# Gate weight tiles placed between the steps of the second attention, with two shared PSUM banks

## The reference

```python
z = hn @ w_in
q_a, k_a, v_a, q_b, k_b, v_b, f_logit, g_a, g_b = jnp.split(z, split_idx, axis=-1)
a = moba_attention(...)            # 8 heads; over 256 tokens causal, with a bias linear in distance
bfx = forgetting_attention(...)    # 8 heads; causal, bias from the cumulated log forget gate
a = merge_heads(a) @ w_proj_a
bfx = merge_heads(bfx) @ w_proj_b
merged = jax.nn.sigmoid(g_a) * a + jax.nn.sigmoid(g_b) * bfx
x = x + merged @ w_out
```

## Time and profile before

| | us |
|---|---|
| median of 3 runs | 3013.37 |
| lowest, highest | 3007.05, 3026.69 |
| the profiled execution | 3013.09 |
| its span | 3011.3 |
| TensorE busy | 2830.1 |
| VectorE busy | 1782.6 |
| ScalarE busy | 1153.4 |

### The profile page before, as it was taken

One profiled execution on the slowest core, in us unless ns is written; L12 is line 12 of the kernel. 1 busy time (PEld: TensorE's weight loads), 2 busy tenths in 40 slices (PEclk: granted clock), 3 DMA queues, 4 the chain that ended last, 5 costly groups with the idle time before them and its releaser, 6 DMA issues.

```text
span 3011.3 us, 33804 instructions
## 1 busy us (share of the span) xinstructions
PE 2830.1 (94%) x12624; PEld 2270.3 (75%) x12624; DVE 1782.6 (59%) x1999; ACT 1153.4 (38%) x1487; POOL 398.4 (13%) x299
## 2 busy tenths in 40 slices
PE   5899998879899999999989998999999999999997
PEld 2477777558778888888767886788787888888886
DVE  2368883475688755555574445545454565556565
ACT  2122222344434444444343444444344444434443
POOL 1215530000377400000070000000000000000000
PEclk9999999899999999999999999999999999999998
DMA  8778783116677655555536551465555565655552
GB/s 308 283 237 303 266 304 123 42 56 214 231 251 265 236 185 193 187 189 192 171 126 222 190 192 38 168 196 194 168 182 168 194 196 181 195 187 188 188 189 98
DMA packets 279977, 579.30 MB, mean 192 GB/s; under 512 B 9585, under 2 KB 12368, under 8 KB 277336
## 3 DMA queue, kind: packets, MB, share of 16 engines
q1 hardware_dynamic: 272128, 540.71, 53.9%
q0 software_dynamic: 7440, 37.43, 3.5%
q10 hardware_dynamic: 328, 0.09, 0.0%
HBM read 572.92 MB, written 5.27 MB: 192 GB/s over the span
## 4 chain that ended last, share of the span: by engine, by line
issue 58%; PE 21%; DVE 7%; POOLq 6%; DMA 2%; POOL 2%; ACT 2%; DVEq 2%; ACTq 0%; SPq 0%
PE bank L365 5%; PE bank L366 5%; PE bank L367 5%; DVE proj_ctx L1444 3%; POOLq L2057 2%; PE bank L625 2%; POOLq L2059 2%; DMA w_raw<-in_w_ada 1%; DVE w_lo L361 1%; POOLq L2066 1%; DVEq L1443 1%; POOLq L2064 1%; PE bank L1756 1%; PE bank L658 1%; ACT probs L732 1%
## 5 line engine op out<-in xcount | busy, mean ns | idle before, releaser
L361 DVE TENSOR_TENSOR w_lo<-w_raw,w_hi 128x1024 fp32r<-128x1024 f32 (+1 forms) x856 | 1117.8, 1328 | 652.6 <-ACT w_hi L353 640.3
L353 ACT ACTIVATE w_hi<-w_raw 128x1024 fp32r<-128x1024 f32 (+1 forms) x856 | 891.7, 1054 | 1278.0 <-PE bank L367 1146.4
L365 PE MATMUL bank<-w_hi,xa_hi 128*128 128x512 f32 (+1 forms) x2304 | 910.3, 395 | 35.9 <-DVE w_lo L361 24.6
L367 PE MATMUL bank<-w_hi,xa_lo 128*128 128x512 f32 (+1 forms) x2304 | 900.2, 391 | 0.0
L366 PE MATMUL bank<-w_lo,xa_hi 128*128 128x512 f32 (+1 forms) x2304 | 900.0, 391 | 0.0
L365 PEld LDWEIGHTS bank<-w_hi,xa_hi 128*128 128x128 f32 x2304 | 436.4, 189 | 148.1 <-issue 32.6
L367 PEld LDWEIGHTS bank<-w_hi,xa_lo 128*128 128x128 f32 x2304 | 435.7, 189 | 90.5
L366 PEld LDWEIGHTS bank<-w_lo,xa_hi 128*128 128x128 f32 x2304 | 436.7, 190 | 88.1 <-issue 0.7
L365 PE MATMUL bank<-w_hi,ffn_act_hi 128*128 128x512 f32 x864 | 339.3, 393 | 7.8 <-DVE w_lo L361 7.8
L366 PE MATMUL bank<-w_lo,ffn_act_hi 128*128 128x512 f32 x864 | 338.1, 391 | 0.0
L367 PE MATMUL bank<-w_hi,ffn_act_lo 128*128 128x512 f32 x864 | 338.0, 391 | 0.0
(11 more groups left out here) (283 smaller groups left out, 1904.2 us busy)
## 6 DMA issues: line engine op xcount, KB each, us to landing
w_raw<-in_w_in SPq DMA_DIRECT2D x116, 1024.0 KB, 5.0
w_raw<-in_w_ada SPq DMA_DIRECT2D x80, 1024.0 KB, 5.8
w_raw<-in_w_up SPq DMA_DIRECT2D x64, 1024.0 KB, 5.2
w_raw<-in_w_down SPq DMA_DIRECT2D x64, 1024.0 KB, 5.1
w_raw<-in_ffn_wg SPq DMA_DIRECT2D x44, 1024.0 KB, 5.1
w_raw<-in_ffn_wu SPq DMA_DIRECT2D x44, 1024.0 KB, 5.2
w_raw<-in_ffn_wd SPq DMA_DIRECT2D x44, 1024.0 KB, 5.1
w_raw<-in_w_out SPq DMA_DIRECT2D x32, 1024.0 KB, 5.1
```

The lines of the kernel that those rows point to most:

```text
L353: act.activation(whi[:, slot, ks, 0:w], raw[:, q, ks, 0:w], ACT.Copy)\
L361: dve.tensor_tensor(wlo[:, slot, ks, 0:w], raw[:, q, ks, 0:w], whi[:, slot, ks, 0:w].bitcast(F32), ALU.subtract).then_inc(sem("lo_made"), 1)
L365: pe.matmul(out, xh, wh, start=first, stop=False)
L367: return pe.matmul(out, xl, wh, start=False, stop=last)
```

## The change

- The eight tiles of the first quarter of g_a and g_b are taken by halves in steps 0 to 15 of the second attention (`gate_half`), one half a step, between the scores and the transposes of the probabilities. They go to banks 1 and 7.
- To free these, keys and queries of all heads share bank 0, and the outputs of all heads bank 6. So TensorE's transposes of head n wait for the copies of head n-1, not n-2, and the output of a head waits for out_lo of the head before.
- The split of tile 0 stands ahead of step 0 on ScalarE and VectorE, that of tile n/2+1 at the end of the even steps 0 to 12.
- The sigmoids of g_a's quarter are issued by ScalarE at the end of step 8, those of g_b's at the end of step 16; TensorE waits for the former before half tile 8, since g_b uses the same banks.
- In the second attention out_lo goes from the middle of VectorE's step to its head.
- The buffer of gate values moves by 8 KB. `merge(0, True)` keeps only the projection tiles. The first attention (`wide()`) stays as it was.

The core of the diff (what is left out are lines of the sigmoid buffer and of the unchanged first attention):

```diff
-        sig = at("gate_sig", [P, 4, NCH], F32, 160)
+        sig = at("gate_sig", [P, 4, NCH], F32, 168)
...
-            for j in range(k):
+            for j in range(k) if js is None else js:
...
-                return ps[0][:, :] if self.wide() else ps[a % 2][:, 0:SEQ]
+                return ps[0][:, :] if self.wide() else ps[0][:, 0:SEQ]
...
-                return ps[1][:, :] if self.wide() else ps[a % 2][:, SEQ:2 * SEQ]
+                return ps[1][:, :] if self.wide() else ps[0][:, SEQ:2 * SEQ]
...
+            def o_bank(self, d):
+                return ps[6 + d % 2] if self.wide() else ps[6]
...
-                    wait(pe, T + "_qk_copied", A.since(s["a"]))
+                    wait(pe, T + "_qk_copied", s["a"])
...
+                if not A.wide() and n < 2 * 8:
+                    gate_half(pe, U, n // 2, n % 2)
...
-                    wait(pe, T + "_out_lo", d - 1)
-                    o = ps[6 + d % 2]
+                    wait(pe, T + "_out_lo", d - 1 if A.wide() else d)
+                    o = A.o_bank(d)
...
-                if 0 <= q < 3:
+                if 0 <= q < 3 and A.wide():
...
+        GATE_BANKS = (ps[1], ps[7])
+
+        def gate_half(pe, U, u, half):
+
+            if u == 4 and half == 0:
+                pe.wait_ge(sem("gate_sigmoid"), 1)
+            unit(pe, U // 4 + u // 4, u % 4, GATE_BANKS, XA, 4 * (u % 4), u % 4 == 0, u % 4 == 3,
+                 js=(2 * half, 2 * half + 1))
+
+        def next_gate(n):
+
+            return n // 2 + 1 if n % 2 == 0 and n // 2 + 1 < 8 else None
+
+        def sigm_1(act, U, b):
+
+            used(act, U + 4 * b + 4)
+            for tk in range(2):
+                m = act.activation(sig[:, 2 * b + tk, :], GATE_BANKS[tk][:, :], ACT.Sigmoid, scale=stat(RSTD + tk))
+            m.then_inc(sem("gate_sigmoid"), 1)
...
+            if not A.wide():
+                hi(act, U // 4, 0)
...
-                q = next_unit(n, hi_)
+                q = next_unit(n, hi_) if A.wide() else next_gate(n)
                 if q is not None:
-                    hi(act, U // 4, q)
+                    hi(act, U // 4 + q // 4, q % 4)
+                if not A.wide() and n in (8, 16):
+                    sigm_1(act, U, n // 16)
...
+            if not A.wide():
+                lo(dve, U // 4, 0)
             for n in range(lo_, hi_ + 4):
+                if not A.wide():
+                    out_lo(dve, A, n, lo_, hi_)
...
-                for b in range(first, 2):
+                for b in () if first else range(2):
```

More of the change, by code:

```diff
@@ L367, in mm3, with unit @@
             return pe.matmul(out, xl, wh, start=False, stop=last)
-        def unit(pe, u4, q, outs, X, k0, first, last, k=KQ, w=NCH, toks=(0, 1), slot=None, follow=0):
+        def unit(pe, u4, q, outs, X, k0, first, last, k=KQ, w=NCH, toks=(0, 1), slot=None, follow=0, js=None):
             slot = q % 2 if slot is None else slot
-            for j in range(k):
+            for j in range(k) if js is None else js:
                 if j % (k // 2) == 0:
@@ L673, in attn_pe @@
             pe.wait_ge(sem(T + "_out_lo"), 16)
-            pe_next(pe, A, U, k0s, 3)
+            if A.wide():
+                pe_next(pe, A, U, k0s, 3)
+        GATE_BANKS = (ps[1], ps[7])
[11 more added lines that the diff above has]
+            m.then_inc(sem("gate_sigmoid"), 1)
         def pe_next(pe, A, U, k0s, q):
@@ L709, in attn_act @@
                         act.wait_ge(sem(T + "_out"), s["d"] + 1)
-                    act.activation(A.X[0][:, srcs_of(s)["o"], :], ps[6 + s["d"] % 2][:, out_cols(s)],
+                    act.activation(A.X[0][:, srcs_of(s)["o"], :], A.o_bank(s["d"])[:, out_cols(s)],
                                    ACT.Copy).then_inc(sem(T + "_out_hi"), 1)
@@ L743, in attn_act, with out_lo @@
                     m.then_inc(sem("diff_squares"), 1)
-                q = next_unit(n, hi_)
+                q = next_unit(n, hi_) if A.wide() else next_gate(n)
                 if q is not None:
-                    hi(act, U // 4, q)
+                    hi(act, U // 4 + q // 4, q % 4)
+                if not A.wide() and n in (8, 16):
+                    sigm_1(act, U, n // 16)
+        def out_lo(dve, A, n, lo_, hi_):
+            for s in outputs_of(A, n, lo_, hi_):
+                dve.wait_ge(sem(A.tag + "_out_hi"), s["d"] + 1)
+                o = srcs_of(s)["o"]
+                dve.tensor_tensor(A.X[1][:, o, :], A.o_bank(s["d"])[:, out_cols(s)],
+                                  A.X[0][:, o, :].bitcast(F32), ALU.subtract).then_inc(sem(A.tag + "_out_lo"), 1)
         def attn_dve(dve, A, lo_, hi_, U):
@@ L825, in attn_dve @@
                         m.then_inc(sem("diff_normed"), 1)
-                q = next_unit(n, hi_)
+                q = next_unit(n, hi_) if A.wide() else next_gate(n)
                 if q is not None:
-                    lo(dve, U // 4, q)
+                    lo(dve, U // 4 + q // 4, q % 4)
         A1 = Attn("att", STEPS, 4, kT, qT, probs, probsT, XA)
@@ L1350, in merge @@
                 g = 3 * n + U_MRG // 4
[L1351 to L1357, removed]
+                if not first:
+                    for q in range(4):
+                        hi(act, g, q)
+                    hi(act, g + 1, 0)
+                    hi(act, g + 1, 1)
+                    sigm(n, 0)
+                    hi(act, g + 1, 2)
+                    hi(act, g + 1, 3)
                 hi(act, g + 2, 0)
                 hi(act, g + 2, 1)
-                sigm(n, 1)
+                if not first:
+                    sigm(n, 1)
                 hi(act, g + 2, 2)
@@ L1680, in merge @@
                     lo(dve, g, 3)
-                for q in range(4):
-                    lo(dve, g + 1, q)
+                    for q in range(4):
+                        lo(dve, g + 1, q)
                 for q in range(4):
```

## The result

The changed kernel takes 3029.93 us (median of 20 runs, 3015.48 to 3037.62) against 3011.95 us (20 runs) for the kernel before on the same chips. The ratio is 1.0055, with a 95% interval of 1.004 to 1.007: a loss of 12 to 21 us.

A forecast was written before the change was run, and what follows sets the result against it. TensorE, busy 94% of the span, bounds the kernel, but a ScalarE-VectorE loop bounds biased steps. Start about 4, step 8 some 12 and the tail the rest make +16.8 us: 3013.1+16.8=3029.9, about 3030 us; 8-in-10 range 3010 to 3042.

The forecast's parts named there:

- the loop and not TensorE bounds biased steps: Biased steps of the second attention: the ScalarE-VectorE loop takes 12.92 us a pair, against 10.66 us by TensorE.
- Wins half a microsecond a pair: Biased pairs of steps: 4.90 us are added to save 5.44 us later.
- step 8 waits for the sigmoids: Step 8: TensorE waits 9.7 us for banks 1 and 7 to be read by the sigmoids, last in ScalarE's step.
- the half tile at the low clock: Step 8, behind the wait: granted clock about 0.50, so the half tile takes 5.44 instead of 2.72 us.
- The dense forget-gate steps and their zero: Steps 9 to 15: TensorE bounds them at 7.05 us each; 2.72 us added and 2.72 us saved per step.
- The tail: Steps 16 to 19, left without gate tiles beside them: a chain of 19.3 us from step 15's end to the projection tiles.
- about 13 us of idle TensorE: Sign of a right forecast: the tail shows this much TensorE idle time, with granted clock 0.5.
- the third table load: ScalarE's switch back to exponentials in step 9: it lies in a wait for VectorE whatever a switch costs.
- a granted clock under 1 in steps 3 to 7: Sign of a wrong forecast, in the biased steps of the second attention.
- The rival in which it stays low: Low clock through the biased steps: 10.66 us instead of 6.46 each, steps 1 to 8 add 26.3 us, 3056 us; 7%.
- they get denser: Argument against low clock in biased steps: granted clock is 1.00 now with 7.3 of 24.6 us idle, and TensorE idles less.
- Numbers: Closing part of the prediction: chances of over 1% slower (7% and 2%) or faster (3%), 8-in-10 range 3010 to 3042.

The follow-up runs named there:

- e4: Changed kernel with the weight split taken by halves, one a step, in ScalarE's wait for the maximum and on VectorE behind it: 3019.02 us, ratio 1.0012.
- e1: Changed kernel without its gate work in the steps: shared banks and out_lo at the head stay, gate tiles, splits and sigmoids as before: 3024.4 us, ratio 1.0034.
- e2: Changed kernel with the first pair of sigmoids at the head of ScalarE's step 8 instead of its end: 3020.65 us, ratio 1.0019.
- e9: e5 with the last tile of g_b taken whole at the end of step 16, its sigmoids one step later: 3005.51 us, ratio 0.998.
- e8: Changed kernel with only g_a's tiles in steps 1 to 8, g_b's covering the tail, splits by half, out_lo mid-step, transposed probabilities sharing a bank: 2995.83 us, ratio 0.994.
- e3: Changed kernel with a plain copy in place of the four sigmoids of the gates' first quarter: 3024.86 us, ratio 1.0041.
- e5: Changed kernel with the splits by half of e4 and the early first sigmoids of e2: 3008.15 us, ratio 0.9986.
- e0: Kernel before with one part of the change alone, keys and queries of all heads sharing bank 0: 3014.12 us, ratio 0.9994.
- e6: Kernel before with only the split of its first two tail tiles moved, by halves into steps 11 to 14: 3004.56 us, ratio 0.9965.

## Why the prediction was right

**The sign and the sum.** Forecast 3030 us and +16.8; measured 3029.93 us (+18 over the kernel before beside it), local +15.5. That the median agrees to 0.1 us is luck, given runs that lie up to 22 us apart; the local sum and its terms are the test (D(n) is VectorE's start of step n):

| stretch | forecast us | measured us |
|---|---|---|
| first transposes to D(3) | 18.6 | 17.85 |
| steps 3 to 6, two pairs | 25.8 | 25.34 |
| D(7) to the first matmul of half 8 | 14.2 | 14.09 |
| half 8 and the rest of step 8 | 7.3 | 7.01 |
| steps 9 to 15 | 49.4 | 49.64 |
| tail to the first projection tile | 19.3 | 19.72 |
| extra for half clock in the projection tiles | 2.7 | 29.25-26.9=2.35 |

The last row sets the stretch from the first projection tile to the first merged addition against the same one before, 1975.6-1948.7=26.9 us. No term is off by more than 0.8 us. The start was over-estimated by that much, mostly because half tile 0 took 4.6 us and not 5.2: the half clock ended earlier than in the earlier trace rows.

**The steps, one by one.** That the loop and not TensorE bounds biased steps was right: e4 shows it by removing the split from the loop, e1 by adding the shared banks and out_lo's order without any gate work. "Wins half a microsecond a pair" holds: 12.84-8.02=4.82 us are paid for 5.44. That step 8 waits for the sigmoids was right (e2 takes 6.8 us off that wait), and so was the half tile at the low clock: 5.29 us, against 2.90 us at full clock in e2 (1881.23 to the transposes at 1884.13). The dense forget-gate steps and their zero were right; e1 shows that they would have cost 0.61 us each without the gate work to hide the loop. The tail was right in size and as a chain of waits (e9, e8). The forecast's sign of "about 13 us of idle TensorE" was too high: the three waits make 10.8 us of a stretch whose length was forecast well, so the work in it was counted short, not the chain.

**What was wrong.** First, the third table load "lies in a wait for VectorE either way": it stands behind that wait and adds 1.28 us to the chain. It cost nothing in the changed kernel, since step 10 is dense, and about a microsecond in e2. Second, one of my own signs for a wrong forecast did appear, a granted clock under 1 in steps 3 to 7 (changed kernel, columns as above):

```profile
1861.00:1862.00 1.00, 0.75 (x5) 0.75 (x6) 0.93 (x3) 0.00 (x0) 0.00 (x0) 0.85 0.88 276
1862.00:1863.00 1.00, 1.00 (x3) 0.80 (x3) 0.72 (x2) 0.11 (x1) 0.00 (x0) 0.50 1.04 406
```

It rose again between 1865 and 1866. The pair of steps around it, by its maxima, takes 12.83 us and the next one 12.84, so it cost nothing: a biased pair has 2.2 us of room on TensorE. The rival in which it stays low did not happen, but "they get denser" was no safe argument against it. Third, the chances do not add up: 3% is left for something unnamed, while "Numbers" gives 2% and 3% to unnamed causes at the two ends.

**The experiments' forecasts** missed by 1.5 us for e1 (its steps take 4.94 us and not 5.03, and fewer biased steps are lengthened than the seven counted), 1 us for e2 (the table load), 1.2 for e3 (mostly the lengths of low-clock stretches), 1.4 for e4 and 2.1 for e5 (both gained more), and 2 to 4 for e9 (in part the loop in the two steps that lost their gate work). Those for e0, e6 and e8 held within 0.7 us.

**Open.** That the +15.5 splits into shares is only partly shown. The edits overlap: the split also delays the sigmoids, by 3 us of their wait (e4), so the 9.0 and 9.4 us of e2 and e4 are not shares of one sum but nearly so (17.1 together). The forecast's own shares (start about 4, step 8 some 12 us) were not tested as such. Whether the front stages' scatter, which moves the start of this stretch by up to 15 us between profiles, has one cause was not looked into.

## What to carry to other kernels

Work moved into a pipeline costs its preparation too: here the tile's matmuls fitted TensorE's gaps, while the split of its weights lengthened the loop of two other engines that had made those gaps. Place such preparation in the time in which its engine already waits inside the loop, and keep enough independent work for the drain at the pipeline's end, where every wait is bare. When a buffer must be given up, look first at the one whose reader comes before something that the writer waits for anyway (the banks of e0 and e8, against that of e1).

## What was not expected of the hardware

- A table load can stand behind the semaphore wait of the activation that it serves. In the first step that wants exponentials it was taken at once (1830.86 in the kernel before, three microseconds ahead of the maximum); in later steps, which have two semaphore waits in the code and not one, it came only after the maximum (1885.02 in e2, 1898.29 in the changed kernel), and its 1.28 us were on ScalarE's chain. The number of waits is not the whole rule: in e3 the load at 1972.56 was taken ahead of a wait for TensorE that ended at 1974.20, at an activation with two waits in the code. What decides it stays open.
- The granted clock fell to 0.50, which is 1.2 GHz, not only during the waits of 9.4, 6.4 and 4.5 us but also at 1861.7, behind a stretch in which TensorE was busy for 13.0 of 15 us and had just waited 1.89 us; at the 2.54 us wait in e2 it did not. In e1, where TensorE was busy for 23.3 of 33 us in biased steps, its mean was 0.84, with three falls to 0.50; in the same steps of the kernel before, with 17.4 of 24.6 us busy, it was 1.00.
- From the first matmul behind a gap to the return to 2.4 GHz passed 3.8 us in e3 (1884.02), and in the changed kernel 3.9 us (1861.25), 5.4 us (1828.99) and 6.1 us (1886.28).
